# Gate half blocks of a fused encoder trunk moved to other steps of its attentions

## What is computed

```python
z = x @ w_in                      # q, k, v of three branches, and 3 x 1024 gate columns g
o_diff = diff_attention(dq, dk, dv, lam, norm_g, lam_init)  # branch d: 4 heads, two softmaxes each, rms norm
o_dsa  = dsa_attention(sq, sk, sv, iq, ik, iw)              # branch s: 8 heads, top 128 keys
o_fox  = forgetting_attention(fq, fk, fv, log_f)            # branch f: 8 heads, forget terms
gates = sigmoid(g).reshape(B, S, 3, D)
y = gates[:, :, 0] * (o_diff @ w_br[0]) + gates[:, :, 1] * (o_dsa @ w_br[1]) + gates[:, :, 2] * (o_fox @ w_br[2])
return y @ w_o
```

## Time and profile before

| | us |
|---|---|
| median of 3 runs | 2491.82 |
| lowest and highest | 2487.12, 2491.95 |
| profiled execution | 2488.1 |
| its span, first to last instruction | 2486.3 |
| PE busy in the span | 2107.3 (85%) |
| DVE busy | 911.2 (37%) |
| ACT busy | 549.5 (22%) |
| POOL busy | 227.7 (9%) |
| mean granted PE clock | 0.934 of full speed |

### The profile page before, as it was taken

The page is one execution under the profiler, slowest core; times in us unless marked ns, Lnnn a source line. Parts: engine busy times, 40 slices in busy tenths (PEclk is TensorE's granted clock), DMA queues, the critical chain, the costliest instruction groups (busy, mean ns, idle before and its releaser), DMA issues.

```text
span 2486.3 us, 29712 instructions
## 1 busy us (share of the span) xinstructions
PE 2107.3 (85%) x9820; PEld 1191.1 (48%) x9820; DVE 911.2 (37%) x1764; ACT 549.5 (22%) x1168; POOL 227.7 (9%) x369
## 2 busy tenths in 40 slices
PE   4999998999958888788579999999998698778882
PEld 3776775776433223222257767757744232222231
DVE  5765644544331111011268564544434211110114
ACT  2344244143010100000033422533421000000000
POOL 0000001000011111111100000100001111111112
PEclk9999998999979989899879999999999798998996
DMA  5211410413269999999632114114143699999993
GB/s 184 91 69 35 136 68 35 136 69 119 93 238 408 400 413 409 407 417 414 251 124 102 35 68 136 35 69 135 46 175 137 265 400 410 410 407 407 419 410 129
DMA packets 96860, 541.44 MB, mean 218 GB/s; under 512 B 19011, under 2 KB 21827, under 8 KB 72161
## 3 DMA queue, kind: packets, MB, share of 16 engines
q1 hardware_dynamic: 76576, 504.75, 51.3%
q0 software_dynamic: 12864, 25.20, 2.9%
q10 hardware_dynamic: 7296, 9.97, 1.6%
HBM read 524.66 MB, written 23.07 MB: 220 GB/s over the span
## 4 chain that ended last, share of the span: by engine, by line
PE 57%; DMA 20%; DVE 11%; issue 6%; ACT 3%; ACTq 1%; POOL 1%; DVEq 0%; SPq 0%; POOLq 0%
PE ps L895 11%; DMA xslot<-in_w_up 9%; PE ps L637 7%; PE ps L639 7%; PE ps L638 7%; PE ps L911 7%; PE ps L823 5%; PE ps L837 4%; DMA ring<-in_w_up 3%; DMA wslot<-in_w_up 3%; DMA scr<-in_w_up 3%; PE ps L739 2%; PE ps L790 2%; DMA scr<-scr 2%; PE ps L761 2%
## 5 line engine op out<-in xcount | busy, mean ns | idle before, releaser
L1736 DVE TENSOR_TENSOR scr<-scr,ps 64x512 f32<-64x512 f32 x64 | 44.2, 691 | 876.5 <-ACT scr L1215 876.5
L637 PE MATMUL ps<-hT_lo,w_hi 128*128 128x512 f32 (+1 forms) x832 | 339.1, 408 | 22.3 <-DVE w_lo L1273 14.3
L639 PE MATMUL ps<-hT_hi,w_hi 128*128 128x512 f32 (+1 forms) x832 | 327.0, 393 | 0.0
L638 PE MATMUL ps<-hT_hi,w_lo 128*128 128x512 f32 (+1 forms) x832 | 326.2, 392 | 0.0
L895 PE MATMUL ps<-ring,scr 128*64 128x512 f32 x512 | 240.8, 626 | 39.8 <-issue 21.2
L1019 ACT ACTIVATE scr<-ps 128x512 f32<-128x512 f32 (+3 forms) x334 | 151.9, 456 | 503.5 <-PE ps L911 400.0
L896 PE MATMUL ps<-ring,scr 128*64 128x512 f32 x512 | 238.5, 621 | 0.0
L1039 ACT ACTIVATE w_hi<-ring 128x1024 fp32r<-128x1024 f32 x124 | 130.6, 1053 | 392.1 <-PE ps L639 319.6
L1273 DVE TENSOR_TENSOR w_lo<-ring,w_hi 128x1024 fp32r<-128x1024 f32 x124 | 150.8, 1216 | 106.7 <-ACT w_hi L1039 99.5
L637 PEld LDWEIGHTS ps<-hT_lo,w_hi 128*128 128x128 f32 (+1 forms) x832 | 156.8, 188 | 63.7 <-issue 13.9
L823 PE MATMUL ps<-scr,ring 128*128 128x512 f32 x384 | 170.6, 606 | 3.3 <-ACT scr L1019 3.3
(11 more groups left out here) (223 smaller groups left out, 2848.8 us busy)
## 6 DMA issues: line engine op xcount, KB each, us to landing
ring<-in_w_down SPq DMA_DIRECT2D x32, 2048.0 KB, 28.5
ring<-in_w_gate SPq DMA_DIRECT2D x32, 2048.0 KB, 33.6
ring<-in_w_up SPq DMA_DIRECT2D x32, 2048.0 KB, 33.3
ring<-in_w_in SPq DMA_DIRECT2D x30, 2048.0 KB, 8.1
xslot<-in_w_gate SPq DMA_DIRECT2D x16, 2048.0 KB, 32.3
xslot<-in_w_up SPq DMA_DIRECT2D x16, 2048.0 KB, 31.7
xslot<-in_w_down SPq DMA_DIRECT2D x16, 2048.0 KB, 27.6
scr<-in_w_gate SPq DMA_DIRECT2D x8, 2048.0 KB, 30.6
```

The lines of the kernel that those rows point to most:

```text
L637: mm(out, a[0], b[1], start=first, stop=False)
L638: mm(out, a[1], b[0], start=False, stop=False)
L639: return mm(out, a[0], b[0], start=False, stop=last)
```

## The change

A function `gate_half_at(br, n)` says which half, if any, stands in iteration n. In branch d the iterations 3, 7, 11 and 15 have none and the 16 halves end in iteration 19. In f and s the iterations 5, 9 and 13 have none and the halves end in iteration 18. PE, ACT and DVE all use it, so the gate copies and the weight splits move with their half. The number and kind of instructions stay the same.

```diff
@@ -412,6 +412,11 @@
+        def gate_half_at(br, n):
+
+            rests = (3, 7, 11, 15) if br == "d" else (5, 9, 13)
+            return None if n in rests or n >= NSTEP + len(rests) else n - sum(r < n for r in rests)
+
@@ -804,8 +809,8 @@
                             turn_probs(n - 2)
-                        if n < NSTEP:
-                            gate_half(n)
+                        if gate_half_at(br, n) is not None:
+                            gate_half(gate_half_at(br, n))
                         if 3 <= n < NSTEP + 3:
                             values(n - 3)
@@ -1129,9 +1134,10 @@
-                        if n < NSTEP and n % 2:
-                            filled(6, ("g", br, n // 2), l)
-                            copy(gate[:, n // 2, :], 6, bank[6].t)
+                        half = gate_half_at(br, n)
+                        if half is not None and half % 2:
+                            filled(6, ("g", br, half // 2), l)
+                            copy(gate[:, half // 2, :], 6, bank[6].t)
@@ -1147,8 +1153,8 @@
-                        if n < NSTEP and n % 2:
-                            split_to(units[first + min(n // 2 + 2, KD - 1)], l)
+                        if half is not None and half % 2:
+                            split_to(units[first + min(half // 2 + 2, KD - 1)], l)
@@ -1469,8 +1475,9 @@
-                        if 2 <= n < NSTEP and n % 2 == 0:
-                            split_to(units[first + min(n // 2 + 1, KD - 1)], l)
+                        half = gate_half_at(br, n - 1)
+                        if n and half is not None and half % 2:
+                            split_to(units[first + min(half // 2 + 2, KD - 1)], l)
```

## The result

The changed kernel takes 2507.3 us in the median of 4 runs (2505.69 to 2508.34), the kernel before 2490.95 (2487.12 to 2491.95). The ratio of runs on the same chips is 1.0088, with a 95% interval of 1.0072 to 1.0105: slower, by 18 to 26 us. The two medians alone differ by only 16.4 us. The forecast was 2515.0, 26.9 us above the profiled execution of before; the range was 2497 to 2533.

What follows compares the result with a forecast made beforehand. TensorE (PE), with 57% of the chain that ended last, was taken to bound the kernel. 2488.1 + 14.3 (f and s) - 0.6 (d with its output product) + 13.2 (clock falls in d) = 2515.0 us; range 2497 to 2533.

Steps and rivals of the forecast that it cites:

- Parts 1 to 3: Branches f and s: drains gain 0.56 us each, rests wait 1.32 and 1.44 us each; both layers +14.3 us.
- Part 4: Branch d at full clock: waits at the new rests against today's even steps and drain, +1.3 and +2.5 us.
- Part 5: Output product behind d: reached warm, 30.70 and 29.13 us become 27.70, a gain of 3.0 and 1.4.
- Part 6: Rests 2 to 4 of d: the clock falls in each, 2.2 us a fall, +13.2 us; bounds 0 and 24.
- A: Rival: no fall of the clock in d's rests, 2501.8 us; chance 0.27.
- B: Rival: the clock falls in the rests of f and s as well, 12 more falls, 2541 us; chance 0.11.
- the strict reading: Skill's rule that waits between bursts lose full clock, read to cool f and s rests too; not used in the sum.
- C: Rival: faster, the waits at d's rests vanish, 2475 us; chance 0.07.
- point of decision: In C: the change wins once all 20 rests together wait less than 29.6 us, against 43.4 by the walk.
- D: Rival: ACT and DVE catch up in the rests and PE ends as today, within 5 us of 2488; chance 0.05.

Runs made afterwards that it cites:

- e3: Kernel before with rests only in f and s, at narrow steps 4, 8 and 12; d keeps its halves. 0.9992 of the kernel before.
- e4: Changed kernel with ACT's copy of the transposed probabilities moved ahead of the exponentials. 1.0006 of the kernel before.
- e6: Changed kernel with 12 extra narrow matmuls ahead of the transposes of steps 8 and 16 in d. 1.0080 of the kernel before.
- e2: The change in f and s alone, rests at 5, 9 and 13; d as in the kernel before. 1.0069 of the kernel before.
- e9: The changed kernel run once more, as neighbour of e10 on the same chip. 1.0090 of the kernel before.
- e7: Copy first as in e4, f and s rests as in e3, d resting only at 3, its drain half ahead of the transposes. 0.9956 of the kernel before.
- e8: As e7, but d rests at steps 1, 2, 3 and 15, with halves in steps 16 to 19. 0.9951 of the kernel before.
- e11: As e7, but d rests at steps 3 and 15, with the last halves in steps 16 and 17. 0.9945 of the kernel before.
- e10: The same kernel as e6, run beside the changed kernel on one chip. 1.0084 of the kernel before.

## Why the prediction was right, step by step

**The sign and the size.** Forecast 26.9 us, measured 22 by the ratio and by the sum over the attentions. The mechanism held in all its steps; the price of a fall of the clock was mis-sized, and by less the waits in f and s. The top of the range is not its own sum: 2526 and 5 are 2531, not 2533.

**Parts 1 to 3, f and s.** Forecast +14.3, the trace shows +13.5. The wait in f was put at 1.32; by the distance of starts (169.59 against 167.45 + 0.98) it is 1.16, since without a half the values start 0.75 us behind the transposes (166.12 to 166.87) and not 0.58, so that PE comes later to the wait. e3 and e4 show that its cause is the chain named, from both sides: a narrower maximum ahead of it, or the copy out of it, and the wait is gone. The 0.56 us ahead of the last values went as said.

**Part 4, d at full clock.** Forecast +1.3 and +2.5. The attention of layer 1 in e6, in which the clock never fell, took 89.23 us: against the 88.11 and 86.90 of before that is +1.1 and +2.3. The two halves of the wait at the rest of step 7 came as walked: 1.2 at the turned norm and 1.9 at the transposes by the distance of starts, against 1.36 and 1.3 + 0.65 = 1.95.

**Part 5.** The output product behind d takes 27.70 us in both layers, a gain of 3.0 and 1.4, as forecast.

**Part 6, the step that was mis-sized.** The falls came where they were expected, and one more in the first rest of layer 1. But the price of 2.2 us is the mean of what the output product had lost, 3.0 and 1.4, to falls that lasted 13.7 and 6.8 us; the product itself stood at half speed for 6.0 and 2.9 us of them. (The prediction has 6.3 and 3.3, and the clock back at about 421.7; the 0.78 and 0.79 of the earlier trace rows put it at 421.4 and 1643.4.) Behind a rest the clock was back after 3.4 us, and around step 16 PE would have waited for part of that anyway (0.24 us at step 17 of e6, where the clock stayed): 1.36 us a fall, 7 falls, 9.5 us in place of 13.2. Of the 4.8 us by which the forecast stood above the 22.1 of the traces 3.7 are here, 0.8 in f and s, and 0.3 in part 4. That seven falls came where six were counted hid a part of the error by luck: six would have cost 8.2. The bounds (0 to 24) held it.

**The rivals.** A (no fall in d) is out: seven falls. B (falls in f and s) is out: in the traces of after, e2 and e9 no rest of f or s, 36 of them, has a microsecond below full clock, so waits as such don't lose the clock here. The Trainium skill ("TensorE: Matmul & The Clock Gate", section "Loop structure matters more than you think") shows its loss with a long DMA wait between every matmul; the strict reading was the prediction's, and the traces of f and s do not bear it out, while in d the clock fell behind waits of 1.6 to 2.9 us. C is out: the rests waited more than they saved. Its point of decision can be checked, though: e7 cut those waits, and the time fell below that of before; e3, which cut them in f and s alone, can't be told from before. D is out by the ratio.

## What to carry to other kernels

Work that only fills time belongs in the steps where the chain beside it is longest: three rests per attention cost 13 us in f and s at the wide steps and nothing at the narrow ones. In the engine's own order it can cover a wait only if it stands ahead of the instruction that waits; e7, e8 and e11 place it so in the drain of d, but no run shows what that alone is worth. Before taking filler out of a step, walk the chain of the other engines from that step's widest operation to the buffer that it frees; here the filler covered a wait that no profile of before printed. And look at what stands in front of the releasing instruction on its own engine: moving one copy ahead of two exponentials was worth 20 us in the changed kernel, where PE waited for that copy, and 4.5 us in the kernel before, where it did so in the even steps of d alone; moving 20 half blocks cost 22.

## What the runs showed that was not expected

- In f and s the rests, with 1.0 to 1.1 us of empty PE among some five microseconds of narrow matmuls, kept the full clock 36 times of 36 in after, e2 and e9, and 24 times of 24 in e6 and e10. In d the steps with 1.7 us or more of wait, with another wait shortly before or 2.9 us in one piece, lost it 18 times of 18. In between, at step 4 of d with 1.6 us, it fell in 4 of 10, with the same instructions each time: one profile can't say what such a step does.
- With twelve matmuls of 256 columns in bf16, 1.5 us of them, in the wait, the clock stayed in the same steps 8 times of 8.
- The clock stood at its lower level for 13.7 us from the drain of before into L823 (407.8 to 421.4), 7.6 of them in the drain, in which PE kept waiting. Behind a rest that a half followed it was 3.4 us in all seven falls of after, but 6.8 us in the one of e6. What a fall costs depends on how long it lasts and on how much of it PE spends waiting anyway.
- Left open: where the 3 us that e10 gained in d went in the whole time. The projections of s took 67.7 us between the product of d and the first scores in e9 and 69.0 in e10, but before shows 69.0 as well in layer 0, so that this is not tied to the extra matmuls.
